# A hybrid decoder step on one Trainium2 core: the retention samples' query products on four column groups

## What is computed

```python
def step(S, xs):
    qi, ki, vi = xs
    cross = jnp.einsum('bihd,bhde->bihe', qi * q_dec[None, :, :, None], S)
    S = S * c_dec[None, :, None, None] + jnp.einsum('bjhd,bjhe->bhde', ki * k_dec[None, :, :, None], vi)
    return S, cross
```

## Time and profile before

| | |
|---|---|
| time, median of 3 runs | 3049.6 us (3049.14 to 3052.08) |
| the profiled execution, its span | 3050.0 us |
| TensorE busy | 2976.0 us, 98% |
| VectorE busy | 1262.6 us, 41% |
| ScalarE busy | 742.6 us, 24% |
| DMA | 174.50 MB, mean 57 GB/s |
| states loaded, stored | 32 loads and 32 stores of 512 KB, 3.7 and 2.8 us from issue to landing |

### The profile page before, as it was taken

One profiled execution on the slowest core, in us unless ns is written; L12 is line 12 of the kernel. 1 busy time (PEld: TensorE's weight loads), 2 busy tenths in 40 slices (PEclk: granted clock), 3 DMA queues, 4 the chain that ended last, 5 costly groups with the idle time before them and its releaser, 6 DMA issues.

```text
span 3050.0 us, 42635 instructions
## 1 busy us (share of the span) xinstructions
PE 2976.0 (98%) x17496; PEld 2777.9 (91%) x17496; DVE 1262.6 (41%) x1638; ACT 742.6 (24%) x1318; POOL 163.7 (5%) x78
## 2 busy tenths in 40 slices
PE   7999999999999999999999999899899999999999
PEld 7879959968986999999999999689679999999999
DVE  6443443443344633233332355744764233332333
ACT  3131132123123322111222131531553111222111
POOL 2000000000000200000000021211220000000000
PEclk9999999999999999999999999899899999999999
DMA  3122041122213111111111122103001111111111
GB/s 126 64 102 63 29 137 62 45 87 77 64 49 114 42 49 46 45 45 45 45 45 45 45 71 57 45 18 102 19 18 49 46 45 45 45 45 45 45 48 74
DMA packets 91333, 174.50 MB, mean 57 GB/s; under 512 B 9840, under 2 KB 15344, under 8 KB 90416
## 3 DMA queue, kind: packets, MB, share of 16 engines
q1 hardware_dynamic: 89296, 167.40, 17.1%
q10 hardware_dynamic: 1920, 5.41, 0.8%
HBM read 143.83 MB, written 25.56 MB: 56 GB/s over the span
## 4 chain that ended last, share of the span: by engine, by line
PE 92%; DVE 5%; ACT 2%; issue 1%; DMA 0%; ACTq 0%; SPq 0%; DVEq 0%
PE ps L1133 78%; PE ps L1298 2%; PE ps L1275 2%; PE ps L1470 2%; PE ps L1270 2%; PE ps L1444 1%; DVE wlo L701 1%; PE ps L1281 1%; PE ps L1173 1%; PE ps L1457 1%; PE ps L1304 1%; DVE x L738 1%; DVE hlo L708 1%; PE ps L1243 1%; ACT sq L477 1%
## 5 line engine op out<-in xcount | busy, mean ns | idle before, releaser
L1133 PE MATMUL ps<-hhi,whi 128*128 128x352 f32 x2976 | 651.0, 327 | 25.8 <-DVE hlo L708 16.3
L1133 PE MATMUL ps<-hhi,wlo 128*128 128x352 f32 x2976 | 643.5, 324 | 0.0
L1133 PE MATMUL ps<-hlo,whi 128*128 128x352 f32 x2976 | 643.0, 324 | 0.0
L468 ACT CAST whi<-wraw 128x512 fp32r<-128x512 f32 x424 | 261.1, 618 | 1135.2 <-PE ps L1133 1121.7
L701 DVE TENSOR_TENSOR wlo<-wraw,whi 128x512 fp32r<-128x512 f32 x424 | 333.9, 794 | 486.9 <-ACT whi L468 486.9
L1133 PEld LDWEIGHTS ps<-hhi,whi 128*128 128x128 f32 x2976 | 506.9, 190 | 29.7 <-DVE hlo L708 17.8
L1133 PEld LDWEIGHTS ps<-hhi,wlo 128*128 128x128 f32 x2976 | 512.7, 188 | 0.0
L1133 PEld LDWEIGHTS ps<-hlo,whi 128*128 128x128 f32 x2976 | 507.8, 189 | 0.0
L1133 PE MATMUL ps<-ahi,whi 128*128 128x352 f32 x2112 | 460.6, 326 | 9.1 <-DVE alo L1111 6.3
L1133 PE MATMUL ps<-ahi,wlo 128*128 128x352 f32 x2112 | 456.0, 323 | 0.0
L1133 PE MATMUL ps<-alo,whi 128*128 128x352 f32 x2112 | 455.3, 324 | 0.0
(11 more groups left out here) (156 smaller groups left out, 1925.0 us busy)
## 6 DMA issues: line engine op xcount, KB each, us to landing
wraw<-in_weights SPq DMA_DIRECT2D x424, 256.0 KB, 2.6
s<-in_state_in SPq DMA_DIRECT2D x32, 512.0 KB, 3.7
out_state_s<-s SPq DMA_DIRECT2D x32, 512.0 KB, 2.8
zr<-z_a ACTq DMA_DIRECT2D x40, 132.0 KB, 2.4
x<-in_xT SPq DMA_DIRECT2D x8, 528.0 KB, 8.7
rope_tab<-in_tables SPq DMA_DIRECT2D x4, 1056.0 KB, 4.8
out_yT<-x SPq DMA_DIRECT2D x8, 528.0 KB, 2.6
atab<-in_attn_tables SPq DMA_DIRECT2D x2, 1056.0 KB, 5.2
```

Of the source, the lines that this page charges most:

```text
L468: act.copy(whi[:, i % RING, :], wraw[:, i % RING, :]).then_inc(w_hi, 1)
L1133: mm = pe.matmul(ps[:, 3 * (m % 2) + t, 0:TB], a[:, slot, w], b[:, s * KG + k, t * TB:(t + 1) * TB], start=(first and j == 0), stop=(last ...
```

## The change

- The queries of two sequences are multiplied in one go behind every even chunk (`sample_queries`): the four products (two sequences, two halves of the features) go to four groups of 32 array columns and so to the four groups of 32 partitions of bank 7. Each group adds up its four products of a head by itself.
- The rest of `sample_head`, the increment of one sequence's state, stays behind every chunk (`sample_state`).
- Once a head, ScalarE copies bank 7 to SBUF (`o_smp`, after the norm of chunk 6), and after chunk 7 one f32 matmul with a constant matrix of ones on four stacked diagonals adds the four groups (`sample_sum`).
- The zeroed query matrices of all eight sequences are held at once (`q_sel`, 544 columns). POOL zeroes them once at the start; once a head VectorE copies the queries into their places (`spread_queries`). The memset and the copy of each sequence go.
- Four buffers for states in place of three; `k_sel` and `q_sel` lie elsewhere in SBUF; 32 more columns of constants.

```diff
-S0_RING = 3
+S0_RING = 4
...
-C_N = C_SINKS + NPAIR
+C_SUM = C_SINKS + NPAIR
+C_N = C_SUM + NS
...
+            pool.memset(q_sel[:, :], 0.0).then_inc(qsel_zero, 1)
             sum_squares(0)
...
-                for c in range(CH + 1):
+                for c in range(CH):
                     norm_o(h, c)
+                    if c == CH - 2:
+                        act.wait_ge(oq_done, h + 1)
+                        act.copy(o_smp[:, :], ps[:, 7, :]).then_inc(oq_kept, 1)
+                norm_o(h, CH)
                 keep_o(h, CH)
...
                 dve.tensor_scalar(k_sel[:, b % 2, :], f32(k_smp[:, :]), cst[:, C_BM + b:C_BM + b + 1], None, ALU.mult
                                   ).then_inc(sel_ready, 1)
-                link(h, dve.memset(q_sel[:, b % 2, :, :], 0.0))
-                dve.tensor_copy(q_sel[:, b % 2, :, NT * b:NT * b + NT], qk[:, 0:2, SEQ + NT * b:SEQ + NT * b + NT]
-                                ).then_inc(sel_ready, 1)
+
+            def spread_queries(h):
+
+                rows = q_sel[:, :].rearrange("p (b n) -> p b n", b=NB)[:, :, 0:2 * NS]
+                dve.wait_ge(qsel_zero, 1)
+                dve.tensor_copy(rows.rearrange("p b (j n) -> p b j n", j=2)[:, :, :, 0:NT],
+                                qk[:, 0:2, SEQ:TOK].rearrange("p j (b t) -> p b j t", b=NB)).then_inc(qsel_ready, 1)
...
                         dve.tensor_copy(k4[:, :, :, :], qk[:, 2:4, SEQ:TOK].unsqueeze(2).to_broadcast([P, 2, 4, NS])
                                         ).then_inc(four_ready, 1)
+                        spread_queries(h)
...
-            def sample_head(h, b):
-
-                pe.wait_ge(sel_ready, h * (1 + 2 * NB) + (1 + 2 * (b + 1)))
-                pe.wait_ge(s0_in[b % S0_RING], s0_count(h, b) + 16)
-                for j in range(2):
-                    mm = pe.matmul(ps[0:NS, 7, :], q_sel[:, b % 2, j, :], s0[:, b % S0_RING, j, :],
-                                   start=False, stop=(b == NB - 1 and j == 1))
-                if b == NB - 1:
-                    mm.then_inc(o_done, 1)
+            def sample_queries(h, b0):
+
+                pe.wait_ge(qsel_ready, h + 1)
+                for b in (b0, b0 + 1):
+                    pe.wait_ge(s0_in[b % S0_RING], s0_count(h, b) + 16)
+                for b in (b0, b0 + 1):
+                    for j in range(2):
+                        g = 2 * (b - b0) + j
+                        col = (2 * b + j) * NS
+                        mm = pe.matmul(ps[g * NS:(g + 1) * NS, 7, :], q_sel[:, col:col + NS], s0[:, b % S0_RING, j, :],
+                                       start=(b0 == 0 and g > 0), stop=(b0 == NB - 2))
+                if b0 == NB - 2:
+                    mm.then_inc(oq_done, 1)
+
+            def sample_state(h, b):
+
+                pe.wait_ge(sel_ready, h * (1 + NB) + (1 + (b + 1)))
                 pe.wait_ge(s_upd, h * CH + (b + 1))
                 for j in range(2):
                     mm = pe.matmul(ps[:, j, :], k_sel[:, b % 2, j * P:(j + 1) * P], v_smp[:, :],
                                    start=True, stop=True)
                 mm.then_inc(sts_done, 1)
+
+            def sample_sum(h):
+
+                pe.wait_ge(oq_kept, h + 1)
+                pe.matmul(ps[0:NS, 7, :], cst[:, C_SUM:C_SUM + NS], o_smp[:, :], start=True, stop=True
+                          ).then_inc(o_done, 1)
...
                     chunk(h, c)
                     if c == 0:
                         sample_within(h)
-                    sample_head(h, c)
+                    if c % 2 == 0:
+                        sample_queries(h, c)
+                    sample_state(h, c)
+                sample_sum(h)
                 turn_o(h, CH - 1)
...
+    cols[:, C_SUM:C_SUM + NS] = i[:, None] % NS == np.arange(NS)
...
-    nc = _bacc.Bacc("TRN2", target_bir_lowering=False, num_devices=1)
+    nc = _bacc.Bacc("TRN2", target_bir_lowering=False, num_devices=1, dynamic_dma_scratch_size=1024)
```

More of the change, by code:

```diff
@@ L144, in trunk @@
         s0 = at("s0", o_alo, [P, S0_RING, 2, DV], F32)
-        k_sel = at("k_sel", o_alo + S0_RING * 4096, [P, 2, DK], F32R)
-        q_sel = at("q_sel", o_alo + S0_RING * 4096 + 2048, [P, 2, 2, NS], F32)
+        o_sel = o_work + 47776
+        k_sel = at("k_sel", o_sel, [P, 2, DK], F32R)
+        q_sel = at("q_sel", o_sel + 2048, [P, NB * (2 * NS + NT)], F32)
+        o_smp = at("o_smp", o_sel + 4224, [P, DV], F32)
         sq = at("sq", o_work, [P, 2, TOK], F32)
@@ L228, in trunk @@
         sel_ready = sem("sel_ready")
+        qsel_zero = sem("qsel_zero")
+        qsel_ready = sem("qsel_ready")
+        oq_done = sem("oq_done")
+        oq_kept = sem("oq_kept")
         sts_done = sem("sts_done")
@@ L744, in _ @@
                     split(0, -LEAD + 1 + k, -LEAD + 2 + k)
-            N_SEQ = 12 + (CH + 1) + 3 + 2 + NB
+            N_SEQ = 12 + (CH + 1) + 3 + 2
             seq = [0]
@@ L1289, in sample_within @@
                 pe.wait_ge(vs_ready, h + 1)
-                pe.wait_ge(sel_ready, h * (1 + 2 * NB) + 1)
+                pe.wait_ge(sel_ready, h * (1 + NB) + 1)
                 pe.matmul(ps[0:NS, 7, :], sc_smp[:, :], v_smp[:, :], start=True, stop=False)
-            def sample_head(h, b):
-                pe.wait_ge(sel_ready, h * (1 + 2 * NB) + (1 + 2 * (b + 1)))
-                pe.wait_ge(s0_in[b % S0_RING], s0_count(h, b) + 16)
-                for j in range(2):
-                    mm = pe.matmul(ps[0:NS, 7, :], q_sel[:, b % 2, j, :], s0[:, b % S0_RING, j, :],
-                                   start=False, stop=(b == NB - 1 and j == 1))
-                if b == NB - 1:
-                    mm.then_inc(o_done, 1)
+            def sample_queries(h, b0):
[12 more added lines that the diff above has]
+                pe.wait_ge(sel_ready, h * (1 + NB) + (1 + (b + 1)))
                 pe.wait_ge(s_upd, h * CH + (b + 1))
```

## The result

The changed kernel takes 3023.25 us (3020.46 to 3027.83, four runs) beside 3049.55 before: a ratio of 0.9909, 95% interval 0.9898 to 0.9921, so 24 to 31 us faster. The forecast was 3042. The rival called side by side had 3025.

A forecast was written before the change was run, and what follows sets the result against it. TensorE was taken as the bound, busy 2976.0 of 3050.0 us. Four heads, each paying 2.08 us in even chunks and winning 3.90 in odd ones, gave -7.3 us from 3049.6, so 3042; range 3022 to 3053.

The forecast's parts named there:

- side by side: Rival for even chunks' query block: all four column groups run at once, two slots; 24.7 us won, 3025; chance 0.27.
- the five slots: Even chunks' query block on TensorE: neighbouring groups overlap by one record; 2.35 us, 0.52 us more than now; chance 0.43.
- The bounds of the block: Even chunks' query block: eight slots without concurrency, 3.54 us, or two with all four groups at once, 1.07 us.
- the 0.09 for loads: Even chunks' query block: three weight loads for new column groups at 0.03 us each.
- The floor: Chunk end on TensorE waits for VectorE's state update L800, behind L832; at most 0.97 us of a chunk can be won.
- The wait behind the tail: Last chunk: L1133 starts 0.24 us after L800 ends, taken as the price of L1275's wait for L800.
- the select at 911.26: VectorE's L792, ending at 911.60, taken as needed by L1304; costs odd chunks some 0.3 us, still below the limit.
- about 0.4 was named: Sign of being right: in odd chunks TensorE idles some 0.4 us before L1275, which L800 releases.
- The new wait in chunk 0: Chunk 0 needs the states of sequences 0 and 1, not 0 alone; bounds 0 and 0.5 us a head, taken as 0.
- The sum at nothing: TensorE's f32 product in chunk 7, 0.98 us a head, costed at nothing since L1258 waits for ScalarE anyway.
- the fourth buffer at nothing: SP's state loads: sequence 3 loads before the first store, 4 to 7 wait for older stores with more time in hand.
- VectorE's and POOL's edits at nothing: Off the path: VectorE's memsets and copies become one copy a head, bounds 0 and 0.3 us; POOL's memset precedes its work.

The follow-up runs named there:

- experiment 5: Changed kernel with VectorE's update of the sample's state moved ahead of its inverse RMS in chunks 0 to 6; 3010.48 us, ratio 0.9866 to the kernel before.
- twice in turn: Changed kernel with every query product issued twice, all four column groups once and then all four again; 3041.88 us, one run.

## Why the prediction was wrong

- **The step that failed is the five slots of an even chunk's query block**: "if matmuls start in program order, a group's second record waits for its first, and the next group's first record can start only when that second one has started". The runs show no such order between column groups: two slots with four groups, four slots with two groups, and four slots for doubled work in either order. The block is 1.00 us where 2.35 was taken, and an even chunk 7.13 where about 8.4 was forecast.
- The step rested on an inference from the earlier trace rows, records and loads of products on the same columns. They show the order within one group and say nothing of two groups. The bounds of the block, 1.07 and 3.54 us, were near: four groups gave 1.00, which is under the lower bound since the 0.09 for loads was hidden, and one group 3.53. So the size that was forecast, 7.3 us, came out as 26.3.
- On the Trainium skill: by the page "TensorE: Matmul & The Clock Gate", section "Part 3: Packing small matmuls — row/col tiling", matmuls start in program order; doubled work issued group by group, done in four slots, disagrees. The same section's list says that loads overlap running matmuls only across row groups, and here eight loads of 128 rows stand within 0.16 us, beside running matmuls of the same rows; but the section's text before that list names loads to the background weight buffer as a second case, which the prediction left out.
- **The rival side by side was right in mechanism and nearly in size**: 24.7 us worked out, 27.6 measured in the chunks. Even chunks won 0.76 us, as it said, with luck: the block won 0.83, and 0.07 of that went to the slower L1292 behind idle time (experiment 5).
- The floor was right: it gave 0.97 us of gain for an odd chunk, and 1.12 came in chunks 3 and 5, 1.03 in chunks 1 and 7. L816 follows L848 by 0.08 and L1292 follows L816 by 0.15, where chunk 0 and the tail of before had shown 0.11 and 0.24. The wait behind the tail was a bad proxy.
- One reading was wrong and cost nothing: the select at 911.26 is for the next chunk's L1304, not for the one at 913.16. After the change L1329 starts at 890.87, ahead of that chunk's select at 890.99. So the 0.3 us charged for it weren't paid, TensorE was ready earlier, and it idled for 0.74 us where about 0.4 was named.
- Chunk 0 was read from head 3 alone. There and in heads 1 and 2 ScalarE loads a table behind the square, so little is won (0.12). Head 0 has no table load there, and its chunk 0 fell from 7.77 to 7.03. The table load of head 3, before and after:

```profile
904.12 1.28 ACT L520 ACT_TABLE_LOAD   x1
```

```profile
883.88 1.28 ACT L528 ACT_TABLE_LOAD   x1
```

- The new wait in chunk 0, taken at nothing, is there: L1319 starts 0.84 us behind L1308 where L1298 started 0.72 us behind L1291 before, and the second state's last part lands at 883.19, 0.14 us ahead of it. In heads 1 to 3 of the changed kernel it costs nothing, since the chunk ends on VectorE. Where TensorE ends chunk 0 it is paid: 0.09 us in head 0 of this profile (7.03 us, where the second profile has 6.94), and in the experiments up to 0.90 us (head 2, twice in turn). It differs from head to head and run to run.
- The sum at nothing, the fourth buffer at nothing, VectorE's and POOL's edits at nothing: right. The one copy of queries takes 0.19 us a head and the copy of the bank 0.58 on an idle ScalarE.

## What to carry to other kernels

Products with 32 output columns can be given to the four column groups and run beside each other, in both orders that were tried; with equally filled groups, the block took as many slots as one group had records. Groups that hold different numbers of records were not tried. Before counting such a gain, find the engine that ends the chunk next: here a floor of VectorE's order kept 0.9 us of every odd chunk, and a swap of two calls, worth nothing before, gave 12 us after. Where no row shows a concurrency, the two bounds are worth more than an order inferred from rows of another kind.

## What the runs showed of the hardware

- Sixteen f32 records of 512 columns on four column groups took 1.85 to 1.88 us, eight records 1.00 us, where one group took 3.53 us for eight. Without the 0.12 us for the change of columns, that is 0.88 against 3.41 us for the same eight records.
- Matmuls and weight loads of a later group start while earlier records of another group wait. Group by group, the last group's first record stands behind twelve others, and the block still took four slots (1.88 us).
- Going to 32 columns and back costs about 0.1 us with four groups as with one: 1.00 - 0.86 = 0.14 and 3.53 - 3.42 = 0.11 us (0.13 in the other even chunks).
- Two profiles of the same program differ by 8 us of span (3018.7 and 3026.8), and 6.6 us of that stand in the attention stage, where the granted clock was 0.96 and 0.93. Why the clock differs there was not tried.
- The loads of the first three states land one behind another, their last parts at 902.07, 903.40 and 904.93 us in the kernel before. So a pair's second state came in only 0.04 us ahead of the first query block (903.44) there already.
